# Prompt rows scaled by ScalarE and added to by GpSimd; GpSimd's additions and the first tile's sum ahead in the last stage

## The chip, the cores and the metric

The kernel runs on one core of a Trainium2 chip. The metric is the device time of one execution in microseconds (us). A core has five engines that each work through a queue of their own: TensorE (PE, matrix products and transposes), VectorE (DVE), ScalarE (ACT), GpSimd (POOL) and SyncE (SP, which issues most of the DMA transfers). They meet only at semaphores: an instruction can wait for a count and can raise one when it is done. Tensors lie in the 128 partitions of the on-chip memory; matrix results come out in eight banks of PSUM.

## What is computed

The reference is one step of a hybrid decoder layer over 320 tokens: 256 of a new sequence (the prompt) and 64 of eight running ones (the samples). Two recurrent branches are mixed and added to the input; what matters here is what follows, the routed experts:

```python
mod = (jax.nn.silu(c) @ p['w_ada'] + p['b_ada'])[:, None, :]
sh1, sc1, g1, sh2, sc2, g2 = jnp.split(mod, 6, axis=-1)
...
x = x + g1 * mixed
h2 = (rms_norm(x, p['norm2_w']) * (1 + sc2) + sh2).reshape(bt * s, D_MODEL)
comb = route(h2, w_router, router_bias)          # two of 16 experts per token, with weights
y_moe = moe_ffn(h2, comb, p['w_exp_gate'], p['w_exp_up'], p['w_exp_down']).reshape(bt, s, D_MODEL)
x = x + g2 * y_moe
...                                              # and a last rms_norm with final_norm_w
```

The shift `sh2` and the gate `g2` are one vector of 1024 for the whole prompt, and one for each sample.

## The kernel before, in words

All is float32. Until the mixing is done (some 694 us) activations lie feature-major: features in partitions, tokens along the row. 171 weight chunks of 1 MB stream through a ring of six buffers; the order is fixed.

**Dispatch stage.** TensorE ends the mixing product and the router's, and ScalarE takes the root of the mean square (`rst`; per token `r3`, a column). VectorE then runs the routing, a chain of some forty tiny operations, nearly each of which waits for the one before (`step`, `dstep`): scores, best group, first and second expert (`first_largest`), ranks, and row numbers `idx` for the dispatch. Semaphore `s_dsp` counts its later steps: DISPATCH_IDX when `idx` is there, DISPATCH_META when the counts per expert are (all engines wait for these at the branch `few`), DISPATCH_FIRST when `selE` is there, a 0/1 matrix that picks the rows of expert 0. Meanwhile TensorE turns the 320 rows to token-major, in six pieces (`turn_u`; tile t is tokens 0 to 127, 128 to 255 or the samples; two halves of 512 features each), and spreads the shift over the rows with products (`shift_rows`). ScalarE copies the shift rows into `hT`, and VectorE, once `selE` is made, computes row = turned row x r3 + shift, in six operations (L2614). From `hT` GpSimd scatters every row twice to a list in memory sorted by expert (L2097), and TensorE picks expert 0's rows with six products (L1373), so that it can begin before that list is back. ScalarE and VectorE copy the result out, TensorE turns it back, and the first expert's products start (L1407, L1410).

**First expert's end.** The sorted rows come back from memory; TensorE turns five tiles of 128 (`turn_tokens`, L1392), and between them it makes six "late" tiles (`turn_late`, L1362 and L1364): the final norm's weight and the prompt's gate `g2` spread over all partitions (four pieces, eight products each) and the samples' gates (two pieces). ScalarE copies them to `wT` and `gT`.

**Experts.** Sixteen experts run one behind the other, 96 rows each; their results go to memory (`yd`), but for the last expert's.

**Last stage.** GpSimd gathers each token's two result rows (`hT` and `y2`, L2113; `s_y12`). ScalarE weighs the first (`weighted`, L1942) and copies the two halves of the last expert's result (`last_half`, L1948). VectorE multiplies these by the gate (`gated_half`, L2735), adds the second rows (`summed`, L2723), multiplies by the gate (`gated`, L2640) and adds the residual `xT` (`residual_rows`, L2730). TensorE picks the last expert's rows for every token (`picked`, L1467) and adds `hT` for the samples and for tile 1 (`plus`, L1474). The three tiles then pass the final norm (`squared` on ScalarE, `final` on VectorE) and are stored; FINAL is their order.

Of the kernel before, what the change touches and what calls it, by code (L numbers as in the profile page):

```python
# [25 lines left out]
P = 128  # L26
D = 1024
# [103 lines left out]
DISPATCH_META = 10  # L131
DISPATCH_FIRST = DISPATCH_META + 4
DISPATCH_STEPS = DISPATCH_FIRST + 8
TM_EARLY = 6
DISPATCH_SEL = DISPATCH_STEPS + 4
FINAL = [0, 2, 1]
# [15 lines left out]
def build(nc, d):  # L152

    ctx = ExitStack()
    with ctx:
# [115 lines left out]
        gsx = late.take(KT, NSAMP)  # L271
        moe.at = late.width
# [344 lines left out]
        def _(sp):  # L617
# [157 lines left out]
            sp.dma_start(d["conv_new"], ncv[:, :, :]).then_inc(s_out, 16)  # L775
            with sp.If(few(sp)):
# [47 lines left out]
        def _(pe):  # L824
# [466 lines left out]
            def shift_rows():  # L1291
# [39 lines left out]
            for n, copied in ((2, 2), (3, 3), (4, 5), (5, 7)):  # L1331
                pe.wait_ge(s_rta, copied)
                turn_u(n)
# [13 lines left out]
            def turn_late(n):  # L1347
# [3 lines left out]
                elif n:  # L1351
                    pe.wait_ge(s_tmc, n if n < 4 else n - 1)
                if n == 8:
                    pe.wait_ge(s_gsx, 1)
                for k in range(4):
# [14 lines left out]
            for t, (c0, c1, rows) in enumerate(TT):  # L1370
                pe.wait_ge(s_htc, 2 * t + 2)
# [24 lines left out]
            def turn_picks():  # L1396

                pe.wait_ge(s_dsp, DISPATCH_SEL - 1)
                pe.wait_ge(s_tmc, 11)
# [62 lines left out]
            def picked(t, h, last):  # L1462

                c0, c1, rows = TT[t]
                out = (states[:, h], b[4 * h], states[:, 2 + h])[FINAL.index(t)]
# [4 lines left out]
            def plus(t, h):  # L1470

                c0, c1, rows = TT[t]
                out = (states[:, h], b[4 * h], states[:, 2 + h])[FINAL.index(t)]
# [3 lines left out]
            with pe.If(few(pe)):  # L1477
# [3 lines left out]
                def one(e, v):  # L1481
# [31 lines left out]
                pe.wait_ge(s_gm, 2)  # L1513
# [3 lines left out]
            with pe.Else():  # L1517
                for n in range(TM_EARLY, 12):
                    turn_late(n)
                pe.wait_ge(s_hk, 2 * KT + KT + 2)  # L1520
                pe.wait_ge(s_tmc, 12)
# [89 lines left out]
        def _(act):  # L1611
# [223 lines left out]
            act.wait_ge(s_mod, 17)  # L1835
            act.activation(shX.rearrange("p k (s t) -> p k s t", t=ST),
# [1109 lines left out]
```

## Time and profile before

| what | value |
|---|---|
| median of 3 runs | 1011.61 us (1007.61 to 1012.08) |
| the profiled execution | 1015.5 us |
| its span, first to last instruction | 1013.7 us |
| TensorE busy | 977.4 us (96%) |
| VectorE, ScalarE, GpSimd busy | 443.4, 234.5, 144.9 us |
| mean granted clock of TensorE | 0.988 |

The profiled execution is 3.9 us above the median, and its own time is 1.8 us above its span. Busy shares are means over stages that differ; what one stage waits for is read from the chain of waits and the timeline of that stage. The granted clock is a share of 2.4 GHz: 1.00 is 2.4 and 0.50 is 1.2 GHz.

### The profile page before, as it was taken

The page shows a single profiled execution, that of the slowest core. Times are in us where ns is not written, and L with a number is a line of the kernel's source. Part 1 is how long each engine was busy: PE and PEld are TensorE (multiplying, and loading weights), DVE is VectorE, ACT ScalarE, POOL GpSimd, SP SyncE. Part 2 cuts the span into 40 slices and gives each one's busy share as a digit, 9 for nine tenths or more (in the row PEclk, how much of TensorE's full clock was granted, in tenths as well). Part 3 has the DMA queues.
Part 4 walks back from the last instruction along what each step waited for, and adds up shares of the span by engine and source line. Part 5 has one row for each costly group of instructions (what it writes and reads, how often), then busy time and mean ns, then how long its engine had stood idle before and what let it go on. Part 6 is the DMA issues. An engine that isn't in the chain of part 4 may idle for free.

```text
span 1013.7 us, 20366 instructions
## 1 busy us (share of the span) xinstructions
PE 977.4 (96%) x8470; PEld 736.1 (73%) x8470; DVE 443.4 (44%) x1084; ACT 234.5 (23%) x461; POOL 144.9 (14%) x236
## 2 busy tenths in 40 slices
PE   5999999999999999999999999999999999999986
PEld 3667666666666566666666777666699999999961
DVE  3121234676257986656641520125352433423316
ACT  2141222233263322242252300003230111101103
POOL 0000222442020443322400000010200000000020
PEclk9999999999999999999999999999899999999998
DMA  9943345564355655655543633342749999999991
GB/s 378 371 173 124 126 166 154 196 234 165 133 197 199 240 197 184 223 205 207 174 145 124 259 112 118 116 154 96 276 184 382 420 423 421 424 422 423 423 349 60
DMA packets 47027, 237.61 MB, mean 234 GB/s; under 512 B 6672, under 2 KB 11120, under 8 KB 23664
## 3 DMA queue, kind: packets, MB, share of 16 engines
q1 hardware_dynamic: 44992, 230.85, 60.1%
q0 software_dynamic: 1520, 5.34, 1.6%
q8 instruction: 46, 0.75, 0.3%
q10 hardware_dynamic: 448, 0.50, 0.1%
q14 instruction: 21, 0.17, 0.0%
HBM read 212.31 MB, written 24.36 MB: 233 GB/s over the span
## 4 chain that ended last, share of the span: by engine, by line
PE 90%; DVE 4%; DMA 2%; ACT 1%; issue 1%; SPq 0%; POOL 0%; DVEq 0%; POOLq 0%
PE pjB L835 16%; PE pjA L835 15%; PE states L1407 11%; PE pjA L1233 7%; PE pjB L1233 7%; PE states L1410 6%; PE pjA L1407 2%; PE pjB L1407 2%; DMA ring<-in_w 2%; PE states L844 2%; PE pjB L1410 1%; PE pjA L1410 1%; PE bank L970 1%; PE bank L1195 1%; PE states L1212 1%
## 5 line engine op out<-in xcount | busy, mean ns | idle before, releaser
L835 PE MATMUL pjB<-hF,ring 128*128 128x320 f32 x608 | 173.3, 438 | 0.0
L835 PE MATMUL pjA<-hF,ring 128*128 128x320 f32 x608 | 171.9, 436 | 0.5 <-ACT regA L1654 0.5
L1407 PE MATMUL states<-ring,oF 128*32 128x128 f32 x1488 | 165.1, 273 | 0.5 <-DVE oF L2630 0.5
L1410 PE MATMUL states<-ring,oF 128*32 128x384 f32 x1488 | 165.3, 491 | 0.0
L1407 PEld LDWEIGHTS states<-ring,oF 128*32 128x32 f32 x1488 | 162.3, 110 | 0.8 <-issue 0.7
L835 PEld LDWEIGHTS pjA<-hF,ring 128*128 128x128 f32 x608 | 113.2, 190 | 50.6 <-issue 7.0
L835 PEld LDWEIGHTS pjB<-hF,ring 128*128 128x128 f32 x608 | 114.2, 192 | 49.2 <-issue 5.7
L2677 DVE TENSOR_TENSOR oF<-oF,states 128x384 f32<-128x384 f32 x15 | 8.3, 555 | 145.1 <-PE states L1410 145.1
L2707 DVE STREAM_TRANSPOSE hF<-oF 32x96 f32<-32x96 f32 x240 | 64.7, 270 | 4.6
L2403 DVE TENSOR_TENSOR G<-G 128x320 f32<-128x320 f32 x32 | 48.8, 1562 | 0.0
L2009 POOL TENSOR_TENSOR G<-regA,G 128x128 f32<-128x128 f32 (+1 forms) x32 | 19.0, 592 | 193.4 <-ACT G L1710 193.4
L1410 PE MATMUL pjB<-ring,hF 128*32 128x384 f32 x360 | 41.9, 491 | 0.0
L1407 PE MATMUL pjB<-ring,hF 128*32 128x128 f32 x360 | 41.8, 273 | 0.0
L1407 PEld LDWEIGHTS pjB<-ring,hF 128*32 128x32 f32 x360 | 39.3, 110 | 0.0
L1407 PE MATMUL pjA<-ring,hF 128*32 128x128 f32 x336 | 39.0, 273 | 0.2 <-DVE hF L2707 0.2
L1410 PE MATMUL pjA<-ring,hF 128*32 128x384 f32 x336 | 39.2, 491 | 0.0
L1410 PEld LDWEIGHTS states<-ring,oF 128*32 128x32 f32 x1488 | 37.3, 108 | 0.0
L1407 PEld LDWEIGHTS pjA<-ring,hF 128*32 128x32 f32 x336 | 36.6, 110 | 0.8 <-DVE hF L2707 0.8
L2106 POOL DMA_DIRECT2D yd<-hF x1 | 0.6, 637 | 251.6 <-DVE hF L2669 251.6
L1233 PE MATMUL pjA<-xsF,ring 128*128 128x320 f32 x128 | 35.9, 433 | 0.0
L1233 PE MATMUL pjB<-xsF,ring 128*128 128x320 f32 x128 | 35.8, 432 | 0.0
L2081 POOL TENSOR_TENSOR G<-G,bp 128x1024 f32<-128x1024 f32 x16 | 34.5, 2158 | 0.0
(526 smaller groups left out, 1371.2 us busy)
## 6 DMA issues: line engine op xcount, KB each, us to landing
ring<-in_w SPq DMA_DIRECT2D x171, 1024.0 KB, 8.4
G<-in_ss SPq DMA_DIRECT2D x16, 512.0 KB, 4.3
out_ss_new<-G SPq DMA_DIRECT2D x16, 512.0 KB, 2.9
G<-csd SPq DMA_DIRECT2D x16, 320.0 KB, 3.4
G<-in_sg SPq DMA_DIRECT2D x4, 1024.0 KB, 6.4
out_sg_new<-G SPq DMA_DIRECT2D x16, 256.0 KB, 2.8
yd<-hF SPq DMA_DIRECT2D x14, 288.0 KB, 7.2
rF<-in_w SPq DMA_DIRECT2D x2, 1024.0 KB, 10.3
```

The costliest lines, as they stand in the source:

```text
L835: mm = pe.matmul(pj[g % 2][:, 0:T], w[:, k, half * P:half * P + P], hF[:, k, :], start=(k == 0), stop=(k == KT - 1))
L844: mm = pe.matmul(out[q:q + QUAD, 0:256], scF[:, k, :], w[:, k, :], start=(k < 4), stop=(k >= 4), tile_position=(0, q), skip_group_check=True)
L970: mm = pe.matmul(bank[0:rows, c0:c1], left[:, c0:c1], right[:, c0:c1], start=True, stop=True)
L1195: pe.matmul(b[4][64 * j:64 * j + 64, c0:c1], x_[:, t, 64 * j:64 * j + 64], L[:, q % 2, j, c0:c1], start=True, stop=True)
L1212: mm = pe.matmul(upd[c][:, 0:2 * P], bT[rows, 2, g * P:g * P + P], xd[rows, 3:5, :].rearrange("p a c -> p (a c)"), start=True, stop=True, ...
L1233: mm = pe.matmul(pj[half][:, 0:T], w[:, k, half * P:half * P + P], src[:, k0 + k, :], start=(first and k == 0), stop=(last and k == KT - 1 ...
L1407: pe.matmul(bank[CAP:P, c * P:(c + 1) * P], rows(c, True), w[:, WIDE:512], start=first and c == 0, stop=last, tile_position=(0, CAP), skip ...
L1410: mm = pe.matmul(bank[QUAD * c:QUAD * c + QUAD, 0:WIDE], rows(c, False), w[:, 0:WIDE], start=first, stop=last, tile_position=(0, QUAD * c) ...
L2009: pool.tensor_tensor(ol, kl, el, ALU.mult)
L2081: pool.tensor_tensor(byhead(so[:, q % 2]), byhead(sn[:, q % 2]), EB[:, :, hs].unsqueeze(3).to_broadcast([P, NS, 2, HD]), ALU.mult).then_in ...
L2403: dve.tensor_tensor(L[:, q % 2, j, :], L[:, q % 2, j, :], cbm[:, g % 2, 0:T], ALU.mult).then_inc(s_M, 1)
L2707: ins = dve.transpose(actT[to, v, :, rows], actE[at, :].rearrange("p (k f) -> p k f", f=P)[:, :, QUAD * q:QUAD * q + QUAD])
```

## The change

Dispatch stage: the prompt's shift is no longer spread by TensorE. ScalarE writes it (`sd`) and the prompt's gate (`gd`) to memory, element by element, soon after they are computed, and SyncE reads the shift back as `sT`, the same row in all 128 partitions. The four prompt pieces of `hT` are made by ScalarE (turned row x r3, out of PSUM) and then GpSimd (+ `sT`, in place); VectorE keeps the two sample pieces. The three steps that make the counts (`meta`) move behind `selE` and these two.

First expert's end: `gT` (prompt) and `wT` come by two such broadcast reads, the final norm's weight straight from an input; the four spread late pieces go, the samples' two stay.

Last stage: tile 0 is weighed, summed and gated before the last expert's halves are copied; GpSimd adds the residual of tiles 0 and 1; tiles end in the order 0, 1, 2.

```diff
-FINAL = [0, 2, 1]
+FINAL = [0, 1, 2]
+LATE = [0, 1, 2, 3, 4, 5, 10, 11]
...
+        sT = gT[:, 1]
...
                     sp.wait_ge(s_mxv, 24)
                     load_extra(2)
+                    sp.wait_ge(s_x, 16 * 3)
+                    sp.wait_ge(s_ldc, 16 * 3)
+                    sp.dma_start(sT, d["sd"].partition_broadcast(P)).then_inc(s_x, 16)
...
             sp.dma_start(d["conv_new"], ncv[:, :, :]).then_inc(s_out, 16)
+            sp.wait_ge(s_rtq, 2)
+            sp.wait_ge(s_x, 16 * 4)
+            sp.dma_start(gT[:, 0], d["gd"].partition_broadcast(P)).then_inc(s_x, 16)
+            sp.dma_start(wT, d["wfin"].partition_broadcast(P)).then_inc(s_x, 16)
...
-                for k in range(KT):
-                    mm = pe.matmul(b[4 + k // 4][:, k % 4 * P:k % 4 * P + P], mod[:, 24 + k, 0:1].to_broadcast([P, P]), ident,
-                                   start=True, stop=True)
-                mm.then_inc(s_ht, 1)
...
-                    elif n < 10:
-                        col = vec[:, V_FIN + f:V_FIN + f + 1] if n < 8 else mod[:, 40 + f, 0:1]
-                        mm = pe.matmul(tm_bank[n][:, k * P:k * P + P], col.to_broadcast([P, P]), ident, start=True, stop=True)
...
-                pe.wait_ge(s_htc, 2 * t + 2)
+                pe.wait_ge(*((s_ysd, 3), (s_ysd, 5), (s_htc, 6))[t])
...
                             turn_tokens(t)
-                            turn_late(TM_EARLY + t)
-                        turn_late(11)
+                            if t < 2:
+                                turn_late(10 + t)
                         turn_picks()
...
-                pe.wait_ge(s_gm, 2)
+                pe.wait_ge(s_osd, 3)
                 for h in range(2):
                     mm = plus(1, h)
...
             act.wait_ge(s_mod, 17)
+            act.dma_start(d["gd"].rearrange("(k p) -> p k", p=P), mod[:, 40:48, 0], allow_slow_non_contiguous=True).then_inc(s_ldc, 16)
+            act.dma_start(d["sd"].rearrange("(k p) -> p k", p=P), mod[:, 24:32, 0], allow_slow_non_contiguous=True).then_inc(s_ldc, 16)
...
-            for t, half in ((2, 0), (2, 1), (0, 0), (1, 0), (0, 1), (1, 1)):
-                rows = TT[t][2]
-                act.wait_ge(s_ht, 3 if t < 2 else 2)
-                act.activation(hT[0:rows, t, half * 512:half * 512 + 512], (pj if t == 2 else b[4:6])[half][0:rows, :],
-                               ACT.Copy).then_inc(s_rta, 1)
+            act.wait_ge(s_ht, 2)
+            for half in range(2):
+                act.activation(hT[0:NSAMP, 2, half * 512:half * 512 + 512], pj[half][0:NSAMP, :], ACT.Copy).then_inc(s_rta, 1)
+            act.wait_ge(s_rst, 4)
+            for n, (t, half) in enumerate(TURNS[0:4]):
+                act.wait_ge(s_ht, 2 + n if n else 1)
+                act.activation(hT[:, t, half * 512:half * 512 + 512], (b[3], b[0], pj[0], pj[1])[n][:, :], ACT.Copy,
+                               scale=r3[:, t:t + 1]).then_inc(s_rta, 1)
...
+                weighted(0)
                 last_half(0)
-                weighted(0)
+                weighted(1)
                 last_half(1)
-                weighted(1)
                 weighted(2)
...
                 pool.tensor_tensor(acc, acc, rs4[:, 2 + t % 2, :], ALU.add).then_inc(s_nss, 1)
+            pool.wait_ge(s_x, 16 * 4)
+            for n, (t, half) in enumerate(TURNS[0:4]):
+                pool.wait_ge(s_rta, 4 + n)
+                y_ = hT[:, t, half * 512:half * 512 + 512]
+                pool.tensor_tensor(y_, y_, sT[:, half * 512:half * 512 + 512], ALU.add).then_inc(s_ysd, 1)
             pool.wait_ge(s_dsp, DISPATCH_IDX)
...
                                                 ).then_inc(s_y12[t], 16)
+                for t in range(2):
+                    pool.wait_ge(s_cmb, 3 + 2 * t)
+                    pool.tensor_tensor(hT[:, t, :], hT[:, t, :], xT[:, t, :], ALU.add).then_inc(s_osd, 1)
...
-            for n, (t, half) in enumerate(TURNS):
-                rows = TT[t][2]
-                dve.wait_ge(s_ht, 3 + n if n else 1)
-                y_ = hT[0:rows, t, half * 512:half * 512 + 512]
-                dve.scalar_tensor_tensor(y_, (b[3], b[0], pj[0], pj[1], b[4], b[5])[n][0:rows, :], r3[0:rows, t:t + 1], y_,
-                                         ALU.mult, ALU.add).then_inc(s_htc, 1)
+            dve.wait_ge(s_rta, 3)
+            for half in range(2):
+                dve.wait_ge(s_ht, 6 + half)
+                y_ = hT[0:NSAMP, 2, half * 512:half * 512 + 512]
+                dve.scalar_tensor_tensor(y_, b[4 + half][0:NSAMP, :], r3[0:NSAMP, 2:3], y_,
+                                         ALU.mult, ALU.add).then_inc(s_htc, 3)
...
+                rows = summed(0)
+                cm(gated(0, rows))
                 gated_half(0)
-                rows = summed(0)
-                gated_half(1)
-                cm(gated(0, rows))
-                cm.wait()
-                cm(residual_rows(0, rows))
                 rows = summed(1)
                 cm(gated(1, rows))
+                gated_half(1)
                 dve.wait_ge(s_w1, 3)
...
-                cm.wait()
-                residual_rows(1, rows).then_inc(s_gm, 1)
+                dve.wait_ge(s_osd, 2)
                 dve.wait_ge(s_yt, 1)
```

GpSimd's queue behind the sums of squares, before (`G` holds `xT` and `gT`; `regA` holds `hT`; DMA rows are the scatters):

```order
L2092 TENSOR_TENSOR G<-G 128x320 [waits s_sq]
L2092 TENSOR_TENSOR G<-G 128x320 [waits s_nss,s_sq] x5
L2097 DMA xd<-regA,idx 736x1024 [waits s_htc,s_dsp]
L2097 DMA xd<-regA,idx 736x1024
L2097 DMA xd<-regA,idx 736x1024 [waits s_htc]
L2097 DMA xd<-regA,idx 736x1024
L2097 DMA xd<-regA,idx 736x1024 [waits s_htc]
L2097 DMA xd<-regA,idx 736x1024
L535 TENSOR_LOAD meta [waits s_dsp]
```

and now:

```order
L2098 TENSOR_TENSOR G<-G 128x320 [waits s_sq]
L2098 TENSOR_TENSOR G<-G 128x320 [waits s_nss,s_sq] x5
L2103 TENSOR_TENSOR regA<-regA,G 128x512 [waits s_rta,s_x]
L2103 TENSOR_TENSOR regA<-regA,G 128x512 [waits s_rta] x3
L2108 DMA xd<-regA,idx 736x1024 [waits s_ysd,s_dsp]
L2108 DMA xd<-regA,idx 736x1024
L2108 DMA xd<-regA,idx 736x1024 [waits s_ysd]
L2108 DMA xd<-regA,idx 736x1024
L2108 DMA xd<-regA,idx 736x1024 [waits s_htc]
L2108 DMA xd<-regA,idx 736x1024
L537 TENSOR_LOAD meta [waits s_dsp]
```

Four additions stand ahead of the scatters, each behind one of ScalarE's scaled pieces (`s_rta`).

VectorE in the last stage, from the copy of the last expert's activations to the sum that takes in tile 0, before:

```order
L2715 COPY hF<-bank 128x384 [waits s_used,s_rd]
L2735 TENSOR_TENSOR oF<-oF,G 96x512 [waits s_eya]
L2723 SCALAR_TENSOR_TENSOR regA<-xsF,G,regA 128x1024 [waits s_w1]
L2735 TENSOR_TENSOR oF<-oF,G 96x512 [waits s_eya,s_cmb]
L2640 TENSOR_TENSOR regA<-regA,G 128x1024
L2730 TENSOR_TENSOR regA<-regA,G 128x1024 [waits s_cmb]
L2723 SCALAR_TENSOR_TENSOR regA<-xsF,G,regA 128x1024 [waits s_w1]
L2640 TENSOR_TENSOR regA<-regA,G 128x1024 [waits s_cmb]
L2748 SCALAR_TENSOR_TENSOR regA<-xsF,G,regA 64x1024 [waits s_w1]
L2730 TENSOR_TENSOR regA<-regA,G 128x1024 [waits s_cmb]
L2753 TENSOR_TENSOR regA<-states,regA 128x2x4x128 [waits s_yt]
```

and now:

```order
L2729 COPY hF<-bank 128x384 [waits s_used,s_rd]
L2737 SCALAR_TENSOR_TENSOR regA<-xsF,G,regA 128x1024 [waits s_w1]
L2654 TENSOR_TENSOR regA<-regA,G 128x1024 [waits s_cmb]
L2749 TENSOR_TENSOR oF<-oF,G 96x512 [waits s_eya]
L2737 SCALAR_TENSOR_TENSOR regA<-xsF,G,regA 128x1024 [waits s_w1]
L2654 TENSOR_TENSOR regA<-regA,G 128x1024 [waits s_cmb]
L2749 TENSOR_TENSOR oF<-oF,G 96x512 [waits s_eya]
L2762 SCALAR_TENSOR_TENSOR regA<-xsF,G,regA 64x1024 [waits s_w1]
L2766 TENSOR_TENSOR regA<-states,regA 128x2x4x128 [waits s_yt,s_osd]
```

The sum and gate of tile 0 stand first, and the two residual additions (L2730) are gone from this queue, so that two operations fewer stand ahead of L2753, now L2766.

TensorE from the turns of the sample rows (`cst,hF`) over the ranks (`G,cst`) and three late turns (`cst,regA`) to the picking of expert 0's rows (`regA,oF`), before:

```order
L1288 MATMUL states<-cst,hF 64x128 [waits s_rta]
L1288 MATMUL states<-cst,hF 64x128 x3
L1338 MATMUL states<-G,cst 128x64 [waits s_rtv]
L1340 MATMUL states<-G,cst 128x48
L1340 MATMUL states<-G,cst 128x32
L1340 MATMUL states<-G,cst 128x16
L1359 MATMUL states<-cst,regA 128x128 x4
L1359 MATMUL states<-cst,regA 128x128 [waits s_tmc]
L1359 MATMUL states<-cst,regA 128x128 x3
L1359 MATMUL states<-cst,regA 128x128 [waits s_tmc]
L1359 MATMUL states<-cst,regA 128x128 x3
L1373 MATMUL states<-regA,oF 96x512 [waits s_htc,s_dsp]
```

and now:

```order
L1297 MATMUL bank<-cst,hF 64x128 x4
L1297 MATMUL states<-cst,hF 64x128 x4
L1344 MATMUL states<-G,cst 128x64 [waits s_rtv]
L1346 MATMUL states<-G,cst 128x48
L1346 MATMUL states<-G,cst 128x32
L1346 MATMUL states<-G,cst 128x16
L1365 MATMUL states<-cst,regA 128x128 x4
L1365 MATMUL states<-cst,regA 128x128 [waits s_tmc]
L1365 MATMUL states<-cst,regA 128x128 x3
L1365 MATMUL states<-cst,regA 128x128 [waits s_tmc]
L1365 MATMUL states<-cst,regA 128x128 x3
L1376 MATMUL states<-regA,oF 96x512 [waits s_ysd,s_dsp]
```

The sample turns lost their waits for ScalarE's copies; the ranks still wait for the routing (`s_rtv`) and the late turns stand behind the ranks; the picking waits for GpSimd's additions (`s_ysd`) in place of VectorE's operations (`s_htc`).

## Rows read from the trace of the kernel before

**Rows 1.** Who TensorE waited for in 718 to 995 (total us, times, longest us).
```profile
PE bank L1444 <- issue: 2.4, 1, 2.4
```

**Rows 2.** Chain that ended last, dispatch stage (start us, length us, what).
```profile
702.25 0.22 DVE G L2542
703.21 0.22 DVE G L2569
709.71 1.33 DVE regA L2614 x2
711.17 1.99 PE states L1373 x2
```

**Rows 3.** The same chain at the first expert's end.
```profile
722.33 0.49 PE states L1407 x3
733.23 0.59 PE bank L1392 x4
734.25 0.89 PE bank L1362 x8
743.15 0.45 PE states L1407 x3
```

**Rows 4.** Timeline, last stage (start us, length us, engine, line, operation [idle before <-releaser]).
```profile
989.36 1.14 ACT L1942 ACTIVATE regA<-regA,G 128x1024 f32<-128x1024 f32 x1
996.09 1.98 PE L1467 MATMUL states<-oF,G 96*128 96x512 f32 x4
998.45 1.27 DVE L2748 SCALAR_TENSOR_TENSOR regA<-xsF,G,regA 64x1024 f32<-64x1024 f32 x1
999.77 3.05 PE L1474 MATMUL bank<-regA,cst 64*64 64x512 f32 x4 [1.70 <-DVE regA L2748]
1002.86 1.28 DVE L2757 TENSOR_TENSOR regA<-bank,G 64x512 f32<-64x512 f32 x2 [0.87 <-PE bank L1474]
1008.51 1.41 DVE L2651 SCALAR_TENSOR_TENSOR regA<-states,G 128x512 f32<-128x512 f32 x2
```

**Rows 5.** Timeline, dispatch stage.
```profile
700.85 0.58 ACT L1852 ACTIVATE regA<-pjB 64x512 f32<-64x512 f32 x1
704.46 0.63 PE L1288 MATMUL states<-cst,hF 128*64 128x128 f32 x4 [0.35 <-ACT regA L1852]
...
708.57 0.66 PE L1359 MATMUL states<-cst,regA 128*128 128x128 f32 x4 [0.69 <-ACT G L1863]
711.91 1.18 POOL L2097 DMA_INDIRECT xd<-regA,idx  x1 [20.28 <-DVE regA L2614]
```

**Rows 6.** Timeline of GpSimd and VectorE in the scan stage.
```profile
353.41 5.85 POOL L2087 TENSOR_TENSOR oF<-oF,rF 128x2560 f32<-128x2560 f32 x1
353.72 6.54 DVE L2394 TENSOR_SCALAR G<-G,bp 128x128 f32<-128x128 f32 x6
...
403.64 0.61 POOL L2076 TENSOR_TENSOR G<-G 128x256 f32<-128x256 f32 x1
403.68 3.05 DVE L2403 TENSOR_TENSOR G<-G 128x320 f32<-128x320 f32 x2
```

**Rows 7.** Groups by line and form, VectorE and GpSimd (count, busy us, mean ns, idle).
```profile
L2487 DVE TENSOR_TENSOR G<-G,rF 128x320 f32<-128x320 f32 x8 | 3.9, 491 | 0.3
...
L2041 POOL TENSOR_TENSOR regA<-regA 128x640 f32<-128x640 f32 x2 | 3.0, 1534 | 1.6 <-ACT regA L1765 1.6
```

**Rows 8.** Durations of one line (ns min/median/max).
```profile
L2394 DVE TENSOR_SCALAR G<-G,bp x96: 242/274/5627, 341.2 to 496.3; 128x128 f32<-128x128 f32 x64, 128x64 f32<-128x64 f32 x32
```

**Rows 9.** Dispatch stage by stretches (us, busy us by engine, clock, DMA).
```profile
710.00:712.00 2.00, 0.83 (x1) 0.39 (x2) 2.00 (x4) 0.00 (x0) 0.09 (x1) 0.58 0.01 4
...
716.00:718.00 2.00, 2.00 (x4) 0.52 (x3) 0.00 (x0) 0.00 (x0) 1.70 (x2) 0.72 0.91 348
```

**Rows 10.** Page, DMA issues (KB each, median us to landing).
```profile
G<-csd SPq DMA_DIRECT2D x16, 320.0 KB, 3.4
```

**Rows 11.** DMA issues in 0 to 20 us.
```profile
cF<-in_c ACTq DMA_DIRECT2D x1, 36.0 KB, 2.2
```

More of the change, by code:

```diff
@@ L130 @@
 DISPATCH_IDX = 7
-DISPATCH_META = 10
-DISPATCH_FIRST = DISPATCH_META + 4
-DISPATCH_STEPS = DISPATCH_FIRST + 8
+DISPATCH_FIRST = DISPATCH_IDX + 4
+DISPATCH_META = DISPATCH_FIRST + 3
+DISPATCH_STEPS = DISPATCH_META + 8
 TM_EARLY = 6
 DISPATCH_SEL = DISPATCH_STEPS + 4
-FINAL = [0, 2, 1]
+FINAL = [0, 1, 2]
+LATE = [0, 1, 2, 3, 4, 5, 10, 11]
 TURNS = [(0, 0), (0, 1), (1, 0), (1, 1), (2, 0), (2, 1)]
@@ L1330, in _ @@
             turn_u(1)
-            for n, copied in ((2, 2), (3, 3), (4, 5), (5, 7)):
-                pe.wait_ge(s_rta, copied)
+            for n in range(2, 6):
+                if n < 4:
+                    pe.wait_ge(s_rta, n)
                 turn_u(n)
@@ L1351, in turn_late @@
                 elif n:
-                    pe.wait_ge(s_tmc, n if n < 4 else n - 1)
-                if n == 8:
+                    pe.wait_ge(s_tmc, n if n < 4 else n - 5)
+                if n == 10:
                     pe.wait_ge(s_gsx, 1)
@@ L1398, in turn_picks @@
                 pe.wait_ge(s_dsp, DISPATCH_SEL - 1)
-                pe.wait_ge(s_tmc, 11)
+                pe.wait_ge(s_tmc, 8)
                 for t, (c0, c1, rows) in enumerate(TT):
@@ L1464, in picked @@
                 c0, c1, rows = TT[t]
-                out = (states[:, h], b[4 * h], states[:, 2 + h])[FINAL.index(t)]
+                out = (states[:, h], states[:, 2 + h], b[4 * h])[t]
                 pe.wait_ge(s_eya if t == 2 else s_eyv, E + h)
@@ L1517, in _ @@
             with pe.Else():
-                for n in range(TM_EARLY, 12):
+                for n in LATE[TM_EARLY:]:
                     turn_late(n)
                 pe.wait_ge(s_hk, 2 * KT + KT + 2)
-                pe.wait_ge(s_tmc, 12)
+                pe.wait_ge(s_tmc, 8)
                 for t, (c0, c1, rows) in enumerate(TT):
@@ L1859, in copy_late @@
                 t, half = divmod(n, 2)
-                act.wait_ge(s_tm, n + 1)
+                act.wait_ge(s_tm, LATE.index(n) + 1)
                 rows = TT[t][2] if n < 6 else NSAMP if n >= 10 else P
-                dst = xT[:, t] if n < 6 else wT if n < 8 else gT[:, t - 4]
+                dst = xT[:, t] if n < 6 else gT[:, t - 4]
                 act.activation(dst[0:rows, half * 512:half * 512 + 512], tm_bank[n][0:rows, :], ACT.Copy).then_inc(s_tmc, 1)
@@ L1902, in one @@
                             copy_tokens(t)
-                            copy_late(TM_EARLY + t)
+                            copy_late(10 + t)
                         act.wait_ge(s_htc, 8)
@@ L1908, in one @@
                             copy_tokens(t)
-                            copy_late(TM_EARLY + t)
-                        copy_late(11)
                         act.wait_ge(s_htc, 6 + XROWS // P)
@@ L1958, in _ @@
                     rows = TT[t][2]
-                    act.wait_ge(s_yt if t == 1 else s_x3, n + 1)
+                    act.wait_ge(*((s_x3, 1), (s_yt, 3), (s_x3, 2))[t])
                     squared(n, t, rows, states[:, 2:4, :].rearrange("p h c -> p (h c)") if t == 1 else hT[0:rows, t, :])
             with act.Else():
-                for n in range(TM_EARLY, 12):
+                for n in LATE[TM_EARLY:]:
                     copy_late(n)
@@ L2633, in _ @@
                                       ALU.is_equal, ALU.mult))
+            dve.wait_ge(s_x, 16 * 6)
             cm = Chain(dve, s_cmb, 1)
@@ L2763, in _ @@
             with dve.Else():
-                dve.wait_ge(s_ht, 8)
+                dve.wait_ge(s_ht, 7)
                 dve.reciprocal(rst[:, :], rst[:, :]).then_inc(s_rst, 1)
@@ L2773, in _ @@
                 hm(dve.tensor_tensor(h_, h_, mod[:, 24:32, 1:].unsqueeze(3).to_broadcast([P, KT, NS, ST]), ALU.add))
-                dve.wait_ge(s_tm, 12)
+                dve.wait_ge(s_tm, 8)
                 def activated(e, v):
@@ L2915 @@
         "dt_bias": a["dt_bias"][0], "a_log": a["a_log"][0], "router_bias": a["router_bias"],
+        "wfin": a["final_norm_w"].reshape(-1),
         "wr": a["w_router"].reshape(KT, P, E).transpose(1, 0, 2),
@@ L2932 @@
     d["yd"] = nc.dram_tensor("yd", (E - 1, CAP, D), F32, kind="Internal").ap()
+    d["sd"] = nc.dram_tensor("sd", (D,), F32, kind="Internal").ap()
+    d["gd"] = nc.dram_tensor("gd", (D,), F32, kind="Internal").ap()
     d["csd"] = nc.dram_tensor("csd", (HEADS, T), F32, kind="Internal").ap()
```

15 lines of the change are left out of this document (8 added, 7 removed).

## The prediction

> **What bounds the kernel now.** First the list of who TensorE waited for, from the dispatch to the last expert's end: its longest wait is one of 2.4 us [rows 1]. The experts between two serial stretches are thus bound by TensorE, and the end moves by what the stretches before, between and behind them gain or lose. Then the chain of waits in the dispatch stage [rows 2]: it runs over VectorE's tiny routing operations, one each 0.24 us (five from 702.25 to 703.43), then `selE` to 709.71, two row operations (L2614), and TensorE's picking product at 711.17. Further along it [rows 3]: expert 0's products from 722.33, the token turns from 733.23, the next expert at 743.15; nothing but TensorE and one ScalarE copy stands in these 9.92 us. Last the timeline of the last stage [rows 4]: TensorE ends `picked` at 998.07, idles 1.70 us until VectorE has made the samples' sum (998.45 to 999.72), needs 3.05 us for `plus` of the samples, and from its end at 1002.86 VectorE works 7.06 us to the last result at 1009.92.
>
> **The change, part by part.** The sum is made against the profiled execution (1015.5 us, span 1013.7) and then set on the median, 1011.6, which lies 3.9 lower.
>
> *First expert's end.* Four spread pieces go, 0.89 us each on the chain [rows 3]: 3.6 us. What is then late: ScalarE must still copy tiles, two sample pieces (0.6 us each) and expert 1's rows (0.85) between turns; stepping these through, tile 4 waits for tile 2's copy, and the last copy lands 6.7 us after the start instead of 9.9. Term: -3.2. The gate and weight now come by two 512 KB broadcast reads at some 697 us. The nearest such read, 320 KB, lands after 3.4 us [rows 10], so by bytes 5.4, or 11 for both in line: by 708, and their first reader is in the last stage. At nothing.
>
> *Shift and gate to memory.* Two writes of 1024 four-byte elements from ScalarE's queue, at about 575 us. No row shows such a write; the nearest is a read of 288-byte rows, 2.2 us [rows 11]. It spreads 128 rows over 16 DMA engines, so a piece cost one at most 2.2 / 8 = 0.28. From below 2.2 us a write; from above 64 elements per engine at 0.28, 18. Even then both are done by 611, and the read of `sT` behind them comes up in SyncE's queue at 657, for a first use at 702. I take nothing.
>
> *Dispatch stage.* VectorE loses four row operations (it keeps the samples' two) and its three count steps move behind `selE`: 0.7 us less ahead of it. TensorE loses sixteen spread products; the turns, which waited for ScalarE's copies and ended at 705.09 [rows 5], end near 703. ScalarE's copy of the samples' second half ends at 701.43 [rows 5]; the first scaled piece follows by about 702.0, and the others at 0.6 us each. The rows are then no longer what the picking waits for: the third late turn, ending 709.23 [rows 5], and `selE`, at 709.0, are. If nothing else changed, picking began at 709.3: -1.9.
>
> But GpSimd's four additions of 128x512 run from 702.0, in the middle of the routing. Price of one: between 0.61 (128x256) and 1.53 (128x640) [rows 6, 7], on the line between them 1.23; 4.9 for four. And what they do to VectorE: in the scan stage a GpSimd addition of 5.85 us started at 353.41, and the VectorE operations issued at 353.72 took 6.54 us for six [rows 6]; the longest of that line took 5.63, its median 0.27 [rows 8]. Two products of 128x320, 0.49 each where GpSimd rests [rows 7], took 3.05 behind GpSimd's of 128x256 and beside a 128x1024 [rows 6]. So a VectorE operation with both inputs on the chip waits till GpSimd's is done, and then gets one turn before GpSimd's next. Stepped through from 702.25: four additions of 1.23 with one routing operation of 0.2 between each, the free reduction beside one of them, and L2569, which ended at 703.43, ends at 707.8: +4.3. Bounds: 0 if such small operations slip through, 1.9 at 0.61 us an addition, 5.5 at 1.53. I take 4.3, from the row of the same kind (both inputs on the chip). The Trainium skill has this in "SBUF — State Buffer", section "Who interferes with whom": the pair of ports that VectorE and GpSimd share is locked for a whole instruction, not divided. If it were divided, the routing would run at 0.49 to 1.5, a third of its pace, for 4.9 us: +3.3 in place of +4.3. The first case above (5.63 against 5.85) agrees with the lock.
>
> So the ranks begin at 709.3 and `selE` is there at 709.7 - 0.7 + 4.3 = 713.3. Queued behind the ranks on TensorE are the late turns and the picking: with 4.3 they end at 713.5. TensorE has then idled from 703 to 709.3. In the trace the granted clock went to 0.58 in 710 to 712, where TensorE was busy 0.83 of 2.00 us, and recovered only in 716 to 718 (0.72) [rows 9]; at half clock three late turns take 0.35 us more each and the ranks, an estimate, 0.8: 715.4. Picking starts +2.3 to +4.2 late. Its length was 8.5 us, 1.7 for each of four products at half clock and 0.9 for the last two; if the clock has recovered by then, all six take 5.2, 3.3 less. Term: -1.0 to +4.2; between ends that far apart I take +2.3, somewhat above the middle, since the clock recovered late in the nearest row. GpSimd's scatters move with the routing from 711.91 to about 712.7, and the sorted rows land still before they are turned: nothing.
>
> *Last stage.* Tile 0's gathers are issued first of the six and are done before 988; ScalarE weighed it only at 989.36 [rows 4], because it stood behind the first half. Ahead, it leaves VectorE with six operations before the samples' sum in place of seven, two of them done before 988. Stepped through: halves at 990 and 994.2, `picked` ends unchanged at 998.07. GpSimd's two additions cost between 1.53 (128x640) and 5.85 (128x2560) each [rows 6, 7], on the line 2.4; the second blocks the samples' sum, which then ends at 997.5, still ahead of 998.07; at 5.85 it would end at 1001, 1.3 later than before, the unlikely end of the range. `plus` then follows without the 1.70 us of idling, and at full clock, as `picked` (0.5 for each of four instructions against 0.76) [rows 4]: its first half ends at 999.9, not 1002.83. VectorE's 7.06 us behind it lose 0.1 at most: -2.9. The last store is now of 64 rows in place of 128, some -0.3. Term: -3.2.
>
> Sum: -3.2 + 2.3 - 3.2 = -4.1. In the profiled execution 1011.4; on the median 1007.5.
>
> **The rivals.** *GpSimd does not hold the routing up* (+0 for +4.3). For it: the operations are of 12 to 48 columns, and no row shows such a small one beside an addition. Against: the blocked operation of rows 8 lost all of GpSimd's time though it needs 0.27 itself. Then dispatch gives -1.9, up to -5.2 with the clock kept, and the sum is -8.3 to -11.6: 1000 to 1003.3, say 1001.5. Chance 0.20.
>
> *The last stage gives nothing back*: GpSimd's additions take the ports ahead of the half tile and the samples' sum, at the 5.85 end. For it: both run while VectorE has only operations with two inputs on the chip. Against: 2.3 us of room. Then -3.2 becomes 0, and the sum -0.9: 1010.7. Chance 0.17.
>
> *Slower: the half clock outlasts the picking.* Place: TensorE from its idling at 703 into expert 0's products. Picking starts +4.2, all six products at 1.7 cost 1.8 more, the turning back 0.7, and expert 0's products, 10.8 us at full clock [rows 3], take double as long as the clock stays low. With the other terms at -6.4, the sum passes +5 if it stays low for 9.6 us of them, and is +11.1 if for all: 1017 to 1023, say 1018. It decides only if the clock is still half when the picking has run for 10 us; in the trace it recovered 6 us into it. Chance 0.06.
>
> **How the numbers follow.** The forecast (routing blocked, last stage gains) has 0.57; its own range is 1003.5 to 1010: dispatch at -1.0 and at +4.2 gives 1004.2 and 1009.4, and some scatter is added (the three runs lie 4.5 apart). The time is its own: 1007.5. The range for 8 in 10 reaches down into the first rival and up past the second: 999.5 to 1012.5. A measurement of this kernel can tell 0.5%, 5.06 us, from no change: faster is below 1006.55. That takes the first rival and 0.24 of the forecast: 0.44. The slower rival is the whole of slower, 0.06; the rest, 0.50, is the same.
>
> **What would show it.** In the trace after: four GpSimd additions of 1.2 us between 702 and 708, and in the same stretch four routing operations of over 1 us in place of 0.2; `idx` near 712.5; picking between 713.5 and 715.4, and its first products at 1.7 us; expert 0 at 723 to 727; 6.7 us between experts 0 and 1; in the last stage `plus` right behind `picked`, and the last result 9 us behind the end of `picked` in place of 11.9. If routing operations stay at 0.2 us, the forecast is wrong towards 1001.5; if `plus` still waits, towards 1010.7; if `sT` lands after 702, the element writes are mispriced.

## The result and the profile after

The changed kernel takes 1012.95 us (median of 20 executions), the kernel before 1009.84: a ratio of 1.0036, interval 1.0025 to 1.0046. So it is slower by some 3.1 to 3.6 us, where 4.1 us less was forecast. A ratio sets all executions of a run, but for far outliers (one of 2009.08 us in e5, whose median is 1005.07 without it, and one of 1677.35 in e6, 1006.71 without it), against those of the kernel before in the same series, so it need not be the quotient of two medians.

Each kernel's profile is cut into four stretches below, all read from its own timelines: from the first routing product on VectorE (`lg`, L2566 after) to expert 0's first product; from there to VectorE's last final sum of the experts (L2708); to the end of the last down projection (`pjB`); to the end of the last result. "First" is the profile that the prediction was made from, "again" a second profile of the same kernel.

| kernel | routing to expert 0 | experts | last down | last stage |
|---|---|---|---|---|
| before, first | 23.80 | 259.48 | 10.42 | 17.69 |
| before, again | 23.67 | 257.72 | 8.87 | 17.85 |
| after | 26.47 | 254.86 | 8.87 | 21.62 |

Against the second profile: +2.8, -2.9, 0.0, +3.8. The sum, 3.7 us, is near what the times differ by; from the last result to the end of the span, which holds the last store, it is 3.4 us instead of 3.7. The forecast had +2.3, -3.2 and -3.2: its first two terms came, the third has the wrong sign. (The changed kernel's profile is of its slowest execution, 1017.69. It is 2.1 us later than the first one of before already at the first routing product, 700.66 against 698.53. That lag arose in 250 to 300 us, which the change does not touch, where the granted clock was 0.90 against 0.97, and 1.00 in the second profile of before. The stretches above do not contain it.)

First the dispatch: the timeline after, of VectorE and then GpSimd (start us, length us, engine, line, operation [idle before <-releaser]).

```profile
704.15 0.20 DVE L2555 TENSOR_REDUCE G<-G 128x3 f32<-128x48 f32 x1
704.39 1.22 DVE L2556 TENSOR_TENSOR G<-G 128x48 f32<-128x48 f32 x1
705.64 1.19 DVE L2557 TENSOR_TENSOR G<-G,cst 128x48 f32<-128x48 f32 x1
706.86 0.20 DVE L2558 TENSOR_REDUCE G<-G 128x3 f32<-128x48 f32 x1
707.10 0.95 DVE L2559 TENSOR_TENSOR G<-G 128x48 f32<-128x48 f32 x1
708.08 1.19 DVE L2583 SCALAR_TENSOR_TENSOR G<-G 128x48 f32<-128x48 f32 x1
...
704.27 4.93 POOL L2103 TENSOR_TENSOR regA<-regA,G 128x512 f32<-128x512 f32 x4 [10.50 <-DMA G<-in_wfin]
```

Four routing operations that took 0.22 each [rows 2] now take 0.95 to 1.22, one to each of GpSimd's additions of 1.23. The reduction between them, which has one input on the chip, keeps its 0.20. From `lg` to the ranks 10.16 us pass instead of 6.46: the hold-up cost 3.7 us (4.3 was forecast).

The chain of waits after, from the picking to the next expert (start us, length us, what).

```profile
717.25 1.71 PE states L1376 x2
718.96 1.71 PE bank L1376 x2
...
722.38 1.03 PE states L1376 x2
...
727.13 0.49 PE states L1410 x3
...
738.03 0.59 PE bank L1395 x4
...
745.00 0.52 PE states L1410 x3
```

The first two pairs of picking products ran at half clock and the last at full, as the forecast had it. From the first token turn to the next expert 6.97 us remain of 9.92 [rows 3].

Now the last stage: timeline after, by ScalarE, VectorE, GpSimd and TensorE.

```profile
993.13 1.15 ACT L1948 ACTIVATE regA<-regA,G 128x1024 f32<-128x1024 f32 x1 [4.12 <-DMA xsF<-yd,idx]
994.19 0.57 ACT L1954 ACTIVATE oF<-pjB 96x512 f32<-96x512 f32 x1
...
994.32 1.28 DVE L2737 SCALAR_TENSOR_TENSOR regA<-xsF,G,regA 128x1024 f32<-128x1024 f32 x1 [2.61 <-ACT regA L1948]
...
996.78 0.68 DVE L2749 TENSOR_TENSOR oF<-oF,G 96x512 f32<-96x512 f32 x1
997.38 3.35 DVE L2762 SCALAR_TENSOR_TENSOR regA<-xsF,G,regA 64x1024 f32<-64x1024 f32 x1
...
991.20 2.72 POOL L2130 TENSOR_TENSOR regA<-regA,G 128x1024 f32<-128x1024 f32 x1 [3.23 <-DVE regA L2654]
996.94 2.72 POOL L2130 TENSOR_TENSOR regA<-regA,G 128x1024 f32<-128x1024 f32 x1 [3.02 <-DVE regA L2654]
...
997.51 3.78 PE L1470 MATMUL states<-oF,G 96*128 96x512 f32 x4 [1.62 <-DVE oF L2749]
1001.23 3.67 PE L1477 MATMUL bank<-regA,cst 64*64 64x512 f32 x4
1004.83 3.17 PE L1477 MATMUL states<-regA,cst 128*128 128x512 f32 x4
...
1011.21 1.27 DVE L2668 SCALAR_TENSOR_TENSOR regA<-regA,G 64x1024 f32<-64x1024 f32 x1
```

Three things differ from [rows 4]. ScalarE copies the second half only behind tile 1's weighing, which waited for a gather until 993.13. The samples' sum takes 3.35 us beside GpSimd's second addition, not 1.27. And the last picked products take 3.78, not 1.98; the two sums behind them take 3.67 and 3.17, but these were slow before as well (3.05 for the first [rows 4], 3.22 and 3.78 in the second profile). The last result ends at 1012.48, 21.62 us behind the last down projection. The same stretch in windows (us, busy us of PE, PEld, DVE, ACT, POOL with counts, granted clock, DMA share, GB/s):

```profile
996.00:998.00 2.00, 0.49 (x1) 0.49 (x2) 2.00 (x3) 0.28 (x1) 1.06 (x1) 0.75 0.00 0
998.00:1000.00 2.00, 2.00 (x3) 0.69 (x3) 2.00 (x1) 0.00 (x0) 1.66 (x1) 0.50 0.00 0
```

TensorE was busy 0.49 of 2.00 us while it waited for VectorE; then the granted clock is 0.50, 1.2 GHz of 2.4, and `picked` and the sums run through it at double length.

### The profile page after: what moved, and what is told of

Read it like the earlier page. It is cut to its first block, busy times and chain, and to the rows that moved or that the text cites. A ratio compares the mean times of both kernels' runs of the same rounds, so it can differ in the third digit from the quotient of the medians.

```text
span 1015.9 us, 20277 instructions
## 1 busy us (share of the span) xinstructions
PE 976.8 (96%) x8422; PEld 736.1 (72%) x8422; DVE 444.1 (44%) x1078; ACT 232.5 (23%) x457; POOL 155.3 (15%) x242
## 4 chain that ended last, share of the span: by engine, by line
PE 89%; DMA 4%; DVE 3%; ACT 2%; issue 1%; POOL 1%; SPq 0%; ACTq 0%; DVEq 0%; POOLq 0%
PE pjB L844 16%; PE pjA L844 15%; PE states L1410 10%; PE pjA L1242 7%; PE pjB L1242 7%; PE states L1413 5%; PE pjA L1410 2%; PE pjB L1410 2%; DMA ring<-in_w 2%; PE states L853 2%; PE pjB L1413 1%; PE pjA L1413 1%; PE bank L979 1%; PE bank L1204 1%; PE states L1221 1%
## 6 DMA issues: line engine op xcount, KB each, us to landing
rF<-in_w SPq DMA_DIRECT2D x2, 1024.0 KB, 10.1
```

## The experiments

Three causes were open for the last stage: the new *order* (a half tile behind a gather), GpSimd's additions holding VectorE (*ports*), and both together; later the *clock* as what makes the delay dear.

**The order undone** (e1).

```
 ScalarE:  weighted(0) last_half(0) weighted(1) last_half(1) weighted(2)
      ->   last_half(0) weighted(0) last_half(1) weighted(1) weighted(2)
 VectorE:  sum 0, gate 0, half 0, sum 1, gate 1, half 1, samples
      ->   half 0, sum 0, half 1, gate 0, sum 1, gate 1, samples
```

> The changed kernel, with the two half tiles of the last expert first again in the last stage: ScalarE copies half 0, weighs tile 0, copies half 1, weighs tile 1; VectorE multiplies a half tile before each tile's sum. GpSimd keeps its two additions. In the changed kernel's profile the second half's copy stood behind tile 1's weighing, which waited for a gather until 993.13 us: copied at 994.19, 3.3 us after its products were done at 990.86. Theory 'order' (the copy's place alone cost the stage its time): 3 us less than the changed kernel's 1012.95, so 1009.9. Theory 'both in series' (behind the late half stands the samples' sum, which GpSimd's second addition stretched from 1.27 to 3.35 us and which ended at 1000.73, only 0.6 us before the picked products at 1001.3): the half tile comes 3 us earlier, but the samples' sum still ends near 1000.7 and the last result moves by 0.5 to 1 us: 1012.2. Theory 'ports' (GpSimd's additions alone): no gain, 1012.9.

Measured: 1010.92, ratio to before 1.0019 (1.0006 to 1.0031); last stage 19.54. VectorE, GpSimd and TensorE in its timeline:

```profile
989.11 3.25 DVE L2654 TENSOR_TENSOR regA<-regA,G 128x1024 f32<-128x1024 f32 x1
992.29 1.27 DVE L2762 SCALAR_TENSOR_TENSOR regA<-xsF,G,regA 64x1024 f32<-64x1024 f32 x1
...
987.97 3.31 POOL L2130 TENSOR_TENSOR regA<-regA,G 128x1024 f32<-128x1024 f32 x1 [5.53 <-DVE regA L2654]
...
993.61 3.04 PE L1477 MATMUL bank<-regA,cst 64*64 64x512 f32 x4 [2.47 <-DVE regA L2762]
```

2 us came back by the medians, between the theories; the interval and that of the changed kernel overlap a little. The halves were early, but now the first addition held tile 1's gate (3.25 instead of 1.22), and TensorE waited 2.47 us for the samples' sum at the end of VectorE's row. "Both in series" had the right shape and blamed the wrong one of the two additions. It isn't the order alone.

**The two residual additions on VectorE** (e2), order as changed.

```
-pool: for t in range(2): wait; hT[:, t] += xT[:, t]
+dve:  residual_rows(0) behind half 0, residual_rows(1) behind the samples' sum
```

> The changed kernel, with the two residual additions of the last stage on VectorE instead of GpSimd (tile 0's behind the first half tile, tile 1's behind the samples' sum); the order of halves and tiles stays as changed. Theory 'ports': the samples' sum takes 1.3 us instead of 3.35 and the end comes 2 us earlier, 1011. Theory 'order': the second half is still copied behind tile 1's gather, the second picked products still start near 997.5, the end does not move: 1012.9, within 0.5. Theory 'both in series': the samples' sum ends at 998.8 instead of 1000.7, but the picked products end at 1001.3 either way: 0 to 0.6 us less, 1012.6.

Measured: median 1008.61, ratio 1.0007 (0.999 to 1.0025), which is wide: seven of twelve executions took 1006.6 to 1008.7 at a mean clock of 0.988 to 0.993, five 1011.2 to 1016.7 at 0.983 to 0.987. Last stage 15.75 in a profile of the fastest of them, which is 2.1 less than before. Its timeline:

```profile
990.61 1.27 DVE L2761 SCALAR_TENSOR_TENSOR regA<-xsF,G,regA 64x1024 f32<-64x1024 f32 x1
...
990.74 1.98 PE L1470 MATMUL states<-oF,G 96*128 96x512 f32 x4 [1.13 <-DVE oF L2746]
992.66 1.93 PE L1477 MATMUL bank<-regA,cst 64*64 64x512 f32 x4
994.51 1.98 PE L1477 MATMUL states<-regA,cst 128*128 128x512 f32 x4
```

The halves still stand behind a gather, and the stage is the shorter one. So "order" falls as a cause by itself: with the additions gone the same order costs nothing. `plus` follows `picked` without a gap, the clock stayed at 1.00, and the two sums take 3.8 us from start to end, 6.9 in before (b1). That VectorE now does 2.4 us more work is not seen. Whether the new order gains anything is open: the next run, with the old order and no addition on GpSimd either, can't be told from this one by its time.

**The last stage of before on the changed kernel** (e3).

```
 e1's order; FINAL = [0, 2, 1] and its PSUM banks; residual rows on VectorE
```

> The changed kernel with the whole last stage of the kernel before (halves first, VectorE adds the residual rows, samples picked second); the first expert's end and the dispatch stay as changed. Theory 'both in series': half tiles as soon as the last down projection gives them and no addition on GpSimd, so the samples' sum ends near 998 instead of 1000.7 and the last result comes 10.2 us behind it as before, near 1008.3 instead of 1012.5: 4.2 us less, 1008.8. Theory 'order' 3 us less, 1010. Theory 'ports' 2 us less, 1011.

Measured: 1009.37, ratio 0.9997 (0.9982 to 1.0012); last stage 16.82 (17.85 in before), routing to expert 0 25.99. With the last stage undone the kernel is level with before: the stretches add up to -1.6 us (+2.3, -2.9, -1.0), which the interval holds. The -1.0 is between two profiles of the same last stage: here the first of the two sums took 2.18 us, in before 3.22. A difference of 1 us between two single profiles is thus no finding.

**The shift's four additions on VectorE** (e4), last stage as changed.

```
-pool: for the four prompt pieces: hT += sT        # during the routing
+dve:  for the four prompt pieces: hT += sT        # behind selE
```

> The changed kernel, with the four additions of the shift to the prompt's token rows on VectorE, right behind the first expert's selections, instead of on GpSimd during the routing; ScalarE still scales them out of PSUM, the last stage stays as changed. Theory 'hold-up': the routing's operations take 0.2 us again instead of about 1.2 (3.7 us less until the ranks), the first expert's start, which came 2.9 us later than before in the profile, goes back to 0.0 to 0.5 later, and the end moves by as much: 1010. Rival 'paid elsewhere': the weights' DMA (at 1.0 of its share from 775 us on) sets the pace of the experts, so that an earlier start is waited away there: 1012.9.

Measured: 1009.64, ratio 0.9994 (0.9984 to 1.0004): 3.3 us less than the changed kernel. Routing to expert 0 22.69, experts 254.84, last stage 21.80. Its timeline in the dispatch and in the last stage:

```profile
709.54 2.49 DVE L2618 TENSOR_TENSOR regA<-regA,G 128x512 f32<-128x512 f32 x4
...
705.38 0.43 PE L1344 MATMUL states<-G,cst 128*128 128x64 f32 x2 [1.98 <-DVE G L2581]
711.24 1.92 PE L1376 MATMUL states<-regA,oF 128*96 128x512 f32 x2
...
987.62 2.45 DVE L2737 SCALAR_TENSOR_TENSOR regA<-xsF,G,regA 128x1024 f32<-128x1024 f32 x1 [0.85 <-ACT regA L1948]
991.84 3.36 DVE L2762 SCALAR_TENSOR_TENSOR regA<-xsF,G,regA 64x1024 f32<-64x1024 f32 x1
```

The ranks come 6.45 us behind `lg`, as in before. VectorE does the four additions in 2.49 us, half of GpSimd's 4.93. The experts take as long from the earlier start as from the later one, so "paid elsewhere" falls. Here tile 1's gather landed 1.2 us earlier against the last down projection than in the changed kernel, yet the last stage is as long (21.80, 21.62). Its lateness is not all that costs: here both of VectorE's sums were held, where in the changed kernel tile 1's waited for the gather and took 1.28.

**TensorE kept busy** (e7): GpSimd's additions stay, five useless products fill TensorE's waits.

```
 picked(2, 1);  +3 products ident x xT into a free bank;  picked(0, 1);  picked(1, 1)
 +2 such products;  wait for the samples' sum;  plus(2)
```

> The changed kernel, with three products more on TensorE between the second picked products of the samples and of tile 0, and two more ahead of the samples' sum that it adds (into a PSUM bank that nobody reads any more), so that TensorE waits less for VectorE there; GpSimd keeps its additions. In the profiles with GpSimd's additions TensorE idled 1 to 2.2 us there, its granted clock fell to 0.50, and the last picked products took 3.3 to 3.8 us and the two sums 3.7 and 3.2 to 3.8, against 1.98, 1.93 and 1.98 at 1.00 with the additions on VectorE. Theory 'the clock makes the hold-up dear': at 1.00 these take 2 us each and the end comes about 3.5 us earlier, 1009.5. Theory 'the hold-up alone': the chain goes by VectorE and GpSimd, the end does not move or comes up to 1 us later: 1013 to 1014.

Measured: 1010.31, ratio 1.0008 (0.9994 to 1.0022): 2.6 us less; last stage 18.85. Its timeline:

```profile
989.98 2.84 PE L1511 MATMUL pjA<-G,cst 128*128 128x512 f32 x6
992.66 1.88 PE L1470 MATMUL states<-oF,G 96*128 96x512 f32 x4
...
996.19 1.93 PE L1477 MATMUL bank<-regA,cst 64*64 64x512 f32 x4
998.05 1.98 PE L1477 MATMUL states<-regA,cst 128*128 128x512 f32 x4
...
987.59 2.56 DVE L2741 SCALAR_TENSOR_TENSOR regA<-xsF,G,regA 128x1024 f32<-128x1024 f32 x1 [0.74 <-ACT regA L1952]
991.93 3.37 DVE L2766 SCALAR_TENSOR_TENSOR regA<-xsF,G,regA 64x1024 f32<-64x1024 f32 x1
```

VectorE is still held (2.56, 3.37), but TensorE's products take 1.9 us. The useless work ends late: `plus` begins at 996.19, the samples' sum ended at 995.30. That may be why less than 3.5 us came. "The hold-up alone" falls.

**No addition on GpSimd** (e5: e2 and e4 together).

> The changed kernel with no addition left on GpSimd: the four additions of the shift on VectorE behind the first expert's selections (as in the run that moved these alone, 1009.6), and the two residual additions of the last stage on VectorE (as in the run that moved those alone, 1008.6). Theory 'two separate hold-ups' (each of GpSimd's two groups of additions holds VectorE in its own stage): the gains add up, 3.3 + 4.3 us under 1012.95, so 1005.3; from the first routing product to expert 0's first product 22.7 us instead of 26.5, and from the last down projection's end to the last result 15.8 instead of 21.6. Rival 'one pace' (an earlier start of the experts is given back in the last stage, by a gather or by the clock): no more than the better of the two alone, 1008.5.

Measured: 1005.25, ratio 0.9966 (0.9945 to 0.9986), at the sum of the two gains. Routing to expert 0 21.41, last stage 16.54 (15.75 in e2, whose last stage is the same). The two hold-ups are separate.

**The kernel before again** (b1).

> The kernel before once more, for a second profile. In its first profile the last expert's final sum on VectorE began 1.8 us after its products had ended, and the last down projection's first half ran at half clock (5.19 us instead of 3.6), which none of the other profiles shows. If that belongs to the kernel: again 283 us from the first routing product to that sum and 10.4 from there to the last down projection's end, a time near 1012. If it belongs to that one execution: 281.5 and 8.9, a time near 1009, and from the last down projection's end to the last result 17.7 or less.

Measured: 1009.42; 281.39 us from `lg` to that sum and 8.87 behind it. Its timeline:

```profile
977.09 0.55 DVE L2694 TENSOR_TENSOR oF<-oF,states 128x384 f32<-128x384 f32 x1 [9.92 <-PE states L1410]
...
978.89 3.63 PE L1456 MATMUL pjA<-ring,hF 128*32 128x512 f32 x24 [0.65 <-DVE hF L2715]
993.50 3.22 PE L1474 MATMUL bank<-regA,cst 64*64 64x512 f32 x4 [1.70 <-DVE regA L2748]
```

The wait of 2.4 us at the last expert's end [rows 1] was of that one execution; the 1.70 us before `plus` and its half clock are of the kernel.

**The second half ahead of tile 1** (e8, on e5), since in e5 its copy waited 2.3 us for tile 1's gather.

```
 ScalarE:  weighted(0) last_half(0) last_half(1) weighted(1) weighted(2)
 VectorE:  sum 0, gate 0, half 0, half 1, residual 0, sum 1, gate 1, samples, residual 1
```

> The run with no addition on GpSimd, with the second half tile of the last expert taken ahead of tile 1: ScalarE copies it before it weighs tile 1's row, VectorE multiplies it right behind the first half. In that run's profile its copy waited for tile 1's gather until 983.51, 2.3 us after its products' end at 981.19, and the picked products behind it ended at 988.95, 0.85 us after the samples' sum at 988.1 that the next products also need. Theory 'the gather holds the second half': the samples' sum now decides, 0.85 us less, 1004.4, and from the last down projection's end to the last result 15.0 to 15.7 us instead of 15.8 to 16.5. Rival 'VectorE sets the stage' (its additions and products follow each other almost without a gap): no change, 1005.3.

Measured: 1003.63, ratio 0.9945 (0.9929 to 0.996), the lowest median of a series here, 0.55% under before. Last stage 15.86 against e5's 16.54, 0.7 less, but no less than e2's 15.75. Its timeline:

```profile
982.37 0.59 ACT L1954 ACTIVATE oF<-pjB 96x512 f32<-96x512 f32 x1 [1.28 <-PE pjB L1459]
...
989.22 1.93 PE L1477 MATMUL bank<-regA,cst 64*64 64x512 f32 x4 [0.48 <-DVE regA L2761]
```

The copy follows the products, and `plus` waits for the samples' sum only. So the gather did hold the second half in e5, by these rows. That freeing it is worth 0.7 us is not shown: two profiles of one last stage, e2 and e5, differ by 0.8, and the intervals of e5 and e8 overlap.

**Three late turns ahead of the ranks** (e6, on e5; e6b is the same kernel for a profile).

```
-ranks; turn_late(0..2); wait selE; picking
+wait logits; turn_late(0..2); ranks; wait selE; picking
```

> As the run with no addition on GpSimd, and the first three of the late transpositions (residual rows, 4 products each) stand ahead of the ranks on TensorE instead of behind them, so that TensorE works while VectorE routes. In the run with the shift on VectorE the ranks' products began 6.45 us behind the first routing product and the picked products 12.31 behind it, each third of the transpositions taking 1.8 us and the picked products 1.71 a pair at half clock. Theory 'idle before the ranks costs the clock': picking starts with the selections and token rows, about 1 us earlier, and its first pairs take 1.0 instead of 1.71: 2 to 3 us less than the run without GpSimd's additions, 1003. Rival 'VectorE sets the picking' (the additions behind the selections end it whatever TensorE does): 0 to 1 us less, 1005.

> The run with three late transpositions ahead of the ranks once more, for a profile: its time was 1007.05 against 1005.25 without that move, where 2 to 3 us less was expected. Theory 'idle before the ranks costs the clock': picking starts less than 11.9 us behind the first routing product, at full clock, and expert 0 less than 21.4. Rival 'VectorE sets the picking': picking starts at 11.5 to 11.9 and expert 0 at 21 to 22. A third, 'the ranks come later': the transpositions, each waiting for ScalarE's copy of the one before, end after the routing does, so that the ranks' products start more than 6.5 us behind the first routing product and everything behind them by as much.

Measured: 1007.05, ratio 0.9976 (0.9959 to 0.9993), then 1002.81 in one execution: no gain over e5 that these show. In the profile picking starts 12.6 us behind `lg` (11.9 in e5), expert 0 22.1 (21.4):

```profile
702.85 0.66 PE L1355 MATMUL states<-cst,regA 128*128 128x128 f32 x4 [0.69 <-ACT G L1870]
703.35 0.33 PE L1366 MATMUL states<-G,cst 128*128 128x64 f32 x2
...
708.38 1.99 PE L1375 MATMUL states<-regA,oF 128*96 128x512 f32 x2 [4.07 <-DVE regA L2614]
```

The routing was done at 702.19; the ranks waited for the third turn until 703.35, the third theory. TensorE then idled 4.07 us for VectorE, and the first pair ran at half clock all the same. The idle time had only moved.

## Why the prediction was wrong

*First expert's end:* right. -2.9 against -3.2; the four spread pieces went and ScalarE's copies were late next, as stepped through.

*Shift, gate and weight to memory:* right at nothing. The bounds of the writes were 2.2 and 18 us; they took 14 to 16, and the shift was on the chip long before 704, as the DMA issues after show (KB each, median us to landing):

```profile
G<-sd SPq DMA_DIRECT2D x1, 512.0 KB, 7.3
...
sd<-mod ACTq DMA_DIRECT2D x1, 4.0 KB, 15.5
```

Written from 572.90, read from 660.08, it was there by 667.4; GpSimd's first addition, at 704.27, began 0.14 us behind ScalarE's first scaled piece (703.46 and 0.67). The read that its row names as releaser counts on the same semaphore, but was issued at 699.05 and took 7.0: it landed later.

*Dispatch:* right, +2.8 in this profile and +2.2 to +2.3 in e1 to e3, for +2.3, which was chosen between -1.0 and +4.2. Picking began 3.7 us late and was 1.1 us shorter from there to expert 0. The hold-up was 3.7 us for 4.3, at 1.23 an addition, as worked out from the line between two rows. That a blocked operation waits GpSimd's whole instruction and then gets one turn is how the rows alternate. The Trainium skill, "SBUF — State Buffer", section "Who interferes with whom", has the pair of ports locked for a whole instruction and the reduction free of it; the 1.22 beside 0.20 above agree. One row that the forecast rests on was read too narrowly: the 5.63 us of [rows 8] are of a TENSOR_SCALAR, with one tensor and a column of numbers (L2394), so not only operations on two tensors are held. None of the operations that the change's own additions held is of that kind.

*Last stage:* here it failed, -3.2 forecast and +3.8 found. The step is "halves at 990 and 994.2, `picked` ends unchanged at 998.07", with "the second blocks the samples' sum, which then ends at 997.5, still ahead of 998.07" and the sentence on `plus` "at full clock" that hangs on it. Counted from the end of the last down projection (992.23 in the profile it was read from), that puts the samples' sum's end 5.3 us and the end of `picked` 5.8 us behind. They came 9.9 and 10.4 us behind.

One ground of the error lies in that profile, which has the stall of b1. Its gathers are issued 14.0 us ahead of the end of the projection; in the second profile of before it is 10.8, after 10.1 (the first two lines are of before, the others of after):

```profile
978.19 1.02 POOL L2113 DMA_INDIRECT regA<-yd,idx  x1 [6.66 <-DMA yd<-hF]
988.63 3.60 PE L1456 MATMUL pjB<-ring,hF 128*32 128x512 f32 x24
...
980.79 1.02 POOL L2124 DMA_INDIRECT regA<-yd,idx  x1 [7.35 <-DMA yd<-hF]
987.25 3.61 PE L1459 MATMUL pjB<-ring,hF 128*32 128x512 f32 x24
```

So "Tile 0's gathers ... are done before 988" held by the clock (987.38), but not against the projection: tile 0's sum and gate were to be done 4.2 us ahead of its end and were done 0.3 us behind it. Tile 1's gather came 2.3 us behind it, and the second copy stood behind that.

The -0.3 for the last store, which no row gave, came: 3.7 us became 3.4. The runs divide the other +3.8, each step between two single profiles, which can differ by 1 us for one code:

- The new order by itself: 15.75 (e2) against 17.85 (before): -2.1. The direction was right in this profile, and so was the mechanism: `plus` right behind `picked` and at full clock, the last result 8.7 us behind the end of `picked` (9 was forecast). Only the late half was missed: `picked` ended 7.0 us behind the projection. By the times of e2 and e3 the gain is not shown.
- GpSimd's additions as a hold-up: 18.85 (e7) against 15.75 (e2): +3.1. The price was near (2.72 to 3.33 us each for 2.4). What failed is the count of what they hold: only the second was put on the path, with 2.3 us of room. In e4, e7 and e1 the first held tile 1's sum or gate too (2.45, 2.56 and 3.25 us for 1.22 to 1.28), in e4 and e7 ahead of the half tile that the picking waits for. In the changed kernel's own profile it held neither: it ended at 993.92, and tile 1's row was weighed only at 994.28, so there the late gather took its place.
- The clock: 21.62 against 18.85 (e7): +2.8. The forecast let TensorE idle less and keep full clock; it waited 1.04 and 1.62 us for the late half, ran at 0.50, and the two sums took 6.8 us from start to end instead of 3.8. Rival two (ports ahead of the half tile and the samples' sum) had the mechanism but stopped at "gives nothing back", since it too left the clock out.

-2.1 + 3.1 + 2.8 = +3.8. The medians say 2.6 us for the clock (e7) and 4.3 for hold-up and clock together (e2), the ratios 2.8 and 2.9, with e2's spread as above. Open is where e2's five slower executions lost their clock, since none of them has a profile; it need not be in this stage, as the stretch from 250 to 300 us shows.

## What to carry to other kernels

An addition given to GpSimd is free only where VectorE has nothing with two inputs on the chip for its whole length (by [rows 8] a column counts as one): count every VectorE operation in that window, not only the one on the path now. In a serial tail, price a delay twice, once as waiting and once as the half clock that TensorE's waiting brings to the products behind it. And profile the kernel before twice: here a stall of 1.8 us, with half clock behind it, belonged to one execution, and made room for the gathers that no other profile has.

## What the hardware showed beyond that

The hold-up goes both ways: in e1 GpSimd's first addition began 0.17 us behind VectorE's sum of tile 1 and took 3.31 us, and the gate behind that sum, begun during the addition, took 3.25; they take 2.72 and 1.22 where they are not held. Filling TensorE's waits with useless products paid in itself: 2.6 us by the medians of the changed kernel and e7.
